# One inference layer on one core: the output projection's first operands loaded by the attention stage's SyncE, ahead of its last stores

## The chip, the cores and the metric

The kernel runs on one core of a Trainium2 chip. The metric is the device time in microseconds (us) of one execution; the median of three runs stands for the kernel. The engines are TensorE (PE, its weight loads PEld), VectorE (DVE), ScalarE (ACT), GpSimd (POOL) and SyncE (SP), which only issues transfers (DMAs).

## The reference

One layer of a streaming encoder, for 2048 prompt frames and 64 new frames of a second stream, D = 1024 features, fp32:

```python
h = rms_norm(x, norm_attn)
qa, ka, va, qb, kb, vb = split(h @ w_in)             # QK norm; rotary for mixer B
A = softmax(qa ka^T * s + rel_bias) va               # 8 heads, own 64-chunk and 8 before
B = sink_softmax(qb kb^T * s, sinks) vb              # 8 heads, own 64-chunk and 2 before
x = x + concat(A, B) @ w_out                         # the "combining" stage
gate, up = split(rms_norm(x, norm_ffn) @ w_gate_up)
x = x + (silu(causal_conv3(gate)) * up) @ w_down     # d_ff = 2816
```

## The kernel before

The work runs in four stages, one after the other, and in each the five engines follow programs of their own that meet only in semaphores: `project` (the input projection, to about 465 us of the span), `attend` (the attention, to 903 us), `combine` (output projection, residual and norm, to 1111 us) and `ffn` (to the end). An fp32 operand goes through TensorE as a high and a low part in three products (hi·hi, hi·lo, lo·hi); ScalarE makes the high part, VectorE the low part by a subtraction.

**attend** walks through 17 token tiles n = 0 to 16 of 128 tokens (tile 16 holds the 64 new frames), each with 12 units and 4 groups of heads: groups 0 and 1 are mixer A, 2 and 3 mixer B. For a group PE does the product with the values (L994), spreads the reciprocals of the sums (L999) and so counts `pv_ok` up; DVE copies them (`copy_r`, L1141) and multiplies (`divide`, L1149) into the buffer `o_t[mixer]`, of which there is one for each mixer. Then SP stores that buffer to the DRAM tensor oT (`store(n, mixer)`, L849). `divide` of a mixer's first group of tile n must wait until the store of tile n-1 has landed, since it writes into the same buffer:

```python
if n and g % 2 == 0:
    dve.wait_ge(o_st[mixer], 16 * n)
```

The sums of tile n are finished while the scores of tile n+1 are already under way, so that DVE does the divide of group (16, 0) in step (16, 7), ahead of the maxima (L1117, L1119) of the units from (16, 8) on, which ACT's exponentials wait for. SP's program is a plain list: what stands in it behind a wait or a transfer is issued behind it. At its end stand the four stores (15, A), (15, B), (16, A), (16, B). The stage ends when the last store has landed and all engines have met in a barrier.

In `attend` the values `v` lie in SBUF as 16 tiles of 2560 B in each partition. Mixer A of tile 15 reads value tiles 11 to 15; tile 16 reads only 0 and 1 (the cache and the new frames).

**combine** walks through 3 blocks of 704 tokens (two halves j of 352 each) and 4 pairs i of output tiles. A pair is 96 matmuls of 128x352: 2 output tiles s, 2 halves, 8 slices k, 3 products. The first block's operands come by pieces: `load_half(q, j)` brings two slices of oT for half j (352 KB), `load_w(g)` the two weight tiles of pair g (2 x 512 KB), `load_x(0, q)` the residual (704 KB). ACT and DVE split them in this order: half piece k = 0, weight tile 0, pieces k = 1 to 7, weight tile 1, then the eight pieces of j = 1. The pieces of j = 1 take the place of those of j = 0's neighbours, so SP issues `load_half(q, 1)` as DVE gets through the low parts (`o_lo_ok`), each followed by `load_x(0, q)`, and then the weights of pair 1. In the meantime POOL prepares sums of the feed-forward's weights, with loads and stores of its own on its own queue.

The buffers that combine and ffn share are made by `Carry`: `work` (the oT pieces lie in its upper third), `w_raw`, `small` (gains and a matrix of ones), `x1`, `big`.

Of the kernel before, what the change touches and what calls it, by code (L numbers as in the profile page):

```python
# [20 lines left out]
F32 = mybir.dt.float32  # L21
# [5 lines left out]
P = 128  # L27
# [664 lines left out]
                prep.piece(n)  # L692


def attend(nc, passed, q_a, k_a, qk_b, v_all, ka_cache, kb_cache, va_cache, vb_cache, sinks, oT):

# [17 lines left out]
    with ExitStack() as ctx:  # L714
# [108 lines left out]
        @block.sync  # L823
        def _(sp):
            by_heads = "f (a p) n -> p (f a) n"

            def load(n):
                c, w = place(n)
                load_raw(sp, raw, q_a, k_a, qk_b, c, w, ld)
                sp.dma_start(v[0:w, own_tile(n), :], v_all[c:c + w, :]).then_inc(ld, 16)  # L830

            def load_cache():

                twice(sp, cache[:, 0:KV_A, :], ka_cache.rearrange(by_heads, p=HEAD), cache_ld)
                twice(sp, cache[:, KV_A:, :], kb_cache.rearrange("(a p) n -> p a n", p=HEAD), cache_ld)
                sp.wait_ge(pv_ok, GROUPS * (FULL + 1))
                sp.dma_start(v[:, CACHE, 0:PAIRS_A * P], va_cache).then_inc(cache_ld, 16)
                sp.dma_start(v[:, CACHE, PAIRS_A * P:], vb_cache).then_inc(cache_ld, 16)

            def load_b(n):  # L840
                c, w = place(n)
                twice(sp, raw_b[:, :, 0:w], qk_b[0:PAIRS_B, :, c:c + w].rearrange(by_heads, p=HEAD), ld_b)

            def store(n, mixer):

                c, w = place(n)
# [348 lines left out]

class Carry:

    def __init__(self, nc, ctx):
        m = Memory(nc, ctx, "carry")
        self.big = m.sbuf("big", [P, 2 * KD * BLOCK + 4 * KD * P], F32R)
        self.x1 = m.sbuf("x1", [P, KD, BLOCK])
        self.w_raw = m.sbuf("w_raw", [P, RAW_RING, P])
        self.work = m.sbuf("work", [P, 12 * BLOCK])
        self.small = m.sbuf("small", [P, SMALL[-1]])  # L1210
# [31 lines left out]
        return self.w[:, 8 * P * c:8 * P * (c + 1)].rearrange("p (a k n) -> p a k n", a=2, n=P)  # L1242


def combine(nc, kept, oT, xT, w_o, gains, all_ones, x1T, h2T, h_sums, w_gu,
            prep_range, w_quads, t_gu, t_dn):


# [7 lines left out]
    with ExitStack() as ctx:  # L1256
# [13 lines left out]
        z = [[m.psum(f"z{s}{i}", [P, 512]) for i in range(2)] for s in range(2)]  # L1270
        ms = kept.ms

        const_ld = m.sem("const_ld")
        o_ld, w_ld = ([m.sem(f"{n}{i}") for i in range(2)] for n in ("o_ld", "w_ld"))
        x_ld, half_ld = ([m.sem(f"{n}{c}") for c in range(PAIRS)] for n in ("x_ld", "half_ld"))
# [39 lines left out]
        def _(sp):  # L1315
# [2 lines left out]

            def load_w(g):
                for s in range(2):  # L1320
                    if g:
                        sp.wait_ge(w_lo_ok[s], g)
                    sp.dma_start(w_raw[s][:], w_o[g % PAIRS, s]).then_inc(w_ld[s], 16)

            def load_o(b, q):
# [5 lines left out]
            def load_half(q, j):  # L1331

                n = PAIRS * j + q
                if j:
                    sp.wait_ge(o_lo_ok, 2 * (n - PAIRS + 1))
                cols = slice(j * SUB, (j + 1) * SUB)
                sp.dma_start(half_raw(n), oT[2 * q:2 * q + 2, :, cols].rearrange("k p n -> p k n")).then_inc(half_ld[n % PAIRS], 16)

# [1205 lines left out]
def encoder_step(nc, a):  # L2544

    scratch = {name: nc.dram_tensor(f"{name}_scratch", shape, F32, kind="Internal").ap()
               for name, shape in (("q_a", (4, P, TOKENS)), ("rel_rows", (P, HEADS, 3 * P)), ("oT", (KD, P, TOKENS)),
                                   ("x1T", (KD, P, TOKENS)), ("h2T", (KD, P, TOKENS)))}
    t_gu = nc.dram_tensor("t_gu_scratch", (D_FF // P, 4, P, 2, KD // 2, P), F32, kind="Internal").ap()
    t_dn = [nc.dram_tensor(f"t_dn{p}_scratch", (KD // 2, P, 2, 1, 4, P) if size == 2 else (KD // 2, 4, P, 2, size // 2, P), F32, kind="Internal").ap()  # L2550
            for p, size in enumerate(PART_SIZES)]
    h_sums = nc.dram_tensor("h_sums_scratch", (N_BLOCKS, 4, P, KD // 2, SUB), F32, kind="Internal").ap()
    passing = ExitStack()
# [3 lines left out]
    attend(nc, passed, scratch["q_a"], a["k_a"], a["qk_b"], a["v_all"], a["ka_cache"], a["kb_cache"], a["va_cache"],  # L2557
           a["vb_cache"], a["sinks"], scratch["oT"])
    passing.close()
    with ExitStack() as ctx:  # L2560
        kept = Carry(nc, ctx)
        combine(nc, kept, scratch["oT"], a["xT"], a["w_o"], a["gains_ffn"], a["all_ones"], scratch["x1T"], scratch["h2T"],
                h_sums, a["w_gu"], PREPARED[2], a["w_quads"], t_gu, t_dn)
        ffn(nc, kept, scratch["h2T"], h_sums, scratch["x1T"], a["w_gu"], a["w_dn"], t_gu, t_dn, a["conv"], a["state"],
            a["yT"], a["gate_prompt"], a["gate_sample"])
# [96 lines left out]
```

## Time and profile before

| | |
|---|---|
| median of 3 runs | 2514.19 us (2508.5 to 2514.99) |
| profiled execution | 2510.97 us, its span 2509.1 us |
| busy: PE, DVE, ACT, POOL | 95%, 68%, 46%, 40% |
| mean granted TensorE clock | 0.983 of 2.4 GHz |
| DMA | 578.24 MB, mean 230 GB/s |

Times inside the profile are us from the span's start. "Busy" is the share of the span in which an engine had an instruction under way. A wait is put down to the engine or transfer that released it. The transfers' time to landing runs from the issue to the last completion.

### The profile page before, as it was taken

Reading aid. Unit: us, or ns where it says so; the run is one execution under the profiler, and the core shown is the slowest. Engines: PE = TensorE matmul, PEld = TensorE weight load, DVE = VectorE, ACT = ScalarE, POOL = GpSimd, SP = SyncE. Lnnn points to the kernel's source line nnn. Section 1 sums busy time; section 2 is a strip of 40 time slices with the busy share of each in tenths; the row PEclk is TensorE's granted clock in tenths of the full one; section 3 lists DMA queues with packets and bytes.
Section 4 is the critical chain, followed back from the end, with each engine's and each line's share of the span. In section 5 each row is a group of like instructions: output and inputs, shape, how many; then the busy total and the mean of one; then the engine's idle time right before and its main releaser. Section 6 shows DMA issues by size and latency. Waiting matters only on the chain. (4 is left out here: it accounts for less than half of the span.)

```text
span 2509.1 us, 44859 instructions
## 1 busy us (share of the span) xinstructions
PE 2385.6 (95%) x15773; PEld 2236.7 (89%) x15773; DVE 1706.2 (68%) x3540; ACT 1159.6 (46%) x2656; POOL 992.1 (40%) x1145
## 2 busy tenths in 40 slices
PE   7999999799898979989999999999999999999997
PEld 5888888678787869988999999989999998999997
DVE  7656666576665656777766667777666677676665
ACT  6232332487676743344434344543344454344343
POOL 3888888668988868811310000123000021000001
PEclk9999999899999989999999999999999999999999
DMA  7776776866776668987786666968666686666665
GB/s 258 233 232 204 215 225 188 218 162 176 205 195 177 171 239 307 320 324 275 261 271 221 210 217 227 330 222 294 214 218 213 216 295 234 220 216 211 219 212 176
DMA packets 320939, 578.24 MB, mean 230 GB/s; under 512 B 35474, under 2 KB 168962, under 8 KB 320594
## 3 DMA queue, kind: packets, MB, share of 16 engines
q1 hardware_dynamic: 280560, 425.89, 53.1%
q0 software_dynamic: 39728, 149.36, 18.6%
q8 instruction: 124, 2.03, 0.3%
q14 instruction: 93, 0.76, 0.1%
q10 hardware_dynamic: 434, 0.20, 0.0%
HBM read 444.81 MB, written 132.10 MB: 230 GB/s over the span
## 5 line engine op out<-in xcount | busy, mean ns | idle before, releaser
L2170 PE MATMUL ffn_x<-carry_big 128*128 128x352 f32 x2508 | 457.7, 324 | 12.2 <-PEq L62 5.5
L2170 PEld LDWEIGHTS ffn_x<-carry_big 128*128 128x128 f32 x2508 | 409.6, 189 | 18.6 <-issue 13.6
L2170 PE MATMUL ffn_z<-ffn_h_hi_S,carry_big 128*128 128x352 f32 x1056 | 278.0, 326 | 16.4 <-DVE carry_big L2315 10.0
L366 PE MATMUL project_z<-project_w_hi,project_h_hi 128*128 128x512 f32 (+3 forms) x680 | 256.3, 377 | 14.9 <-DVE project_w_lo L539 11.5
L2069 POOL TENSOR_TENSOR carry_x<-carry_x,carry_work 128x352 f32<-128x352 f32 x48 | 52.2, 1088 | 507.5 <-DVE carry_work L2433 449.1
L366 PE MATMUL project_z<-project_w_lo,project_h_hi 128*128 128x512 f32 (+3 forms) x680 | 252.8, 372 | 0.0
L366 PE MATMUL project_z<-project_w_hi,project_h_lo 128*128 128x512 f32 (+3 forms) x680 | 252.5, 371 | 0.0
L2315 DVE TENSOR_TENSOR carry_big<-carry_w_raw,carry_big 128x512 fp32r<-128x512 f32 (+2 forms) x413 | 227.7, 559 | 0.9 <-ACT carry_big L2251 0.7
L2063 POOL DMA_DIRECT2D carry_work<-h_sums_scratch x8 | 4.4, 554 | 565.5 <-DVE ffn_y_lo_S L2337 561.0
L2170 PEld LDWEIGHTS ffn_z<-ffn_h_hi_S,carry_big 128*128 128x128 f32 x1056 | 188.1, 189 | 22.7 <-DVE carry_big L2315 22.5
L2251 ACT ACTIVATE carry_big<-carry_w_raw 128x512 fp32r<-128x512 f32 (+2 forms) x413 | 196.1, 502 | 6.2 <-PEq L62 4.6
L2170 PE MATMUL ffn_z<-ffn_h_lo_S,carry_big 128*128 128x352 f32 x528 | 170.5, 323 | 0.0
L2208 ACT ACTIVATE carry_work<-ffn_x 128x352 f32<-128x352 f32 x138 | 64.1, 464 | 215.3 <-PE ffn_x L2170 215.1
L366 PEld LDWEIGHTS project_z<-project_w_hi,project_h_hi 128*128 128x128 f32 (+1 forms) x680 | 126.9, 187 | 40.0 <-DVE project_h_lo L532 9.5
L2170 PE MATMUL ffn_x<-ffn_y_hi_S,carry_big 128*128 128x352 f32 x528 | 152.7, 326 | 9.9 <-DVE carry_x L2408 6.2
L2213 ACT ACTIVATE carry_work<-ffn_x 128x352 f32<-128x352 f32 x138 | 64.2, 465 | 203.9 <-PE ffn_x L2170 203.9
L2170 PE MATMUL ffn_z<-ffn_y_hi_S,carry_big 128*128 128x352 f32 x528 | 150.6, 323 | 0.0
L366 PEld LDWEIGHTS project_z<-project_w_hi,project_h_lo 128*128 128x128 f32 (+1 forms) x680 | 126.8, 186 | 24.9 <-issue 0.8
L963 PE MATMUL attend_s<-attend_keys,attend_q_hi 128*128 128x320 f32 (+4 forms) x368 | 134.4, 369 | 14.7 <-DVE attend_q_lo L1157 7.9
L138 POOL TENSOR_TENSOR passed_quads<-passed_quads 128x512 fp32r<-128x512 f32 x110 | 144.7, 1316 | 8.8
L366 PEld LDWEIGHTS project_z<-project_w_lo,project_h_hi 128*128 128x128 f32 (+1 forms) x680 | 127.0, 187 | 22.0 <-issue 0.8
L82 PE MATMUL combine_z<-combine_o_hi,carry_big 128*128 128x352 f32 x512 | 129.5, 333 | 15.2 <-DVE carry_big L1542 12.2
(249 smaller groups left out, 6458.1 us busy)
## 6 DMA issues: line engine op xcount, KB each, us to landing
carry_big<-t_gu_scratch SPq DMA_DIRECT2D x264, 512.0 KB, 4.0
carry_big<-t_dn_scratch SPq DMA_DIRECT2D x240, 256.0 KB, 3.3
carry_w_raw<-w_gu SPq DMA_DIRECT2D x198, 256.0 KB, 4.1
t_gu_scratch<-passed_quads POOLq DMA_DIRECT2D x88, 512.0 KB, 4.8
passed_quads<-w_quads POOLq DMA_DIRECT2D x110, 256.0 KB, 4.4
carry_w_raw<-w_dn SPq DMA_DIRECT2D x180, 128.0 KB, 3.4
carry_w_raw<-w_o SPq DMA_DIRECT2D x24, 512.0 KB, 6.1
t_dn_scratch<-passed_quads POOLq DMA_DIRECT2D x22, 512.0 KB, 4.4
```

The source lines that it names most:

```text
L82: last = nc.tensor.matmul(out, w_parts[w](k), act_parts[a](k), start=(k == 0 and (w, a) == PASSES[0]), stop=(k == n_k - 1 and (w, a) == PA ...
L138: pool.tensor_tensor(lo, four, hi.bitcast(F32), ALU.subtract).then_inc(self.lo_ok, 1)
L366: last = nc.tensor.matmul(z[c][0:w, 0:width], h[:, k, 0:w], ww[:, k, first:first + width], start=(k == 0 and h is hi and ww is w_hi), stop ...
L963: last = nc.tensor.matmul(ps[:, bank, 0:width], q[:, query, :], keys[:, key, c + first:c + first + width], start=q is q_hi and not begun, ...
L2063: pool.dma_start(h_source(b, name), src).then_inc(h_ld[H_STAGE[name]], 16)
L2069: nc.gpsimd.tensor_tensor(total, total, part[:], ALU.add).then_inc(done, 1)
L2170: mm = nc.tensor.matmul(bank[:, 0:SUB], weights(c)[:, wp, k, :], (hi, lo)[a][name][:, 1 if short else k, :], start=first and k == 0 and (w ...
L2208: nc.scalar.activation(sum2[g % 2][:], x_ps[g % 2][:, 0:SUB], ACT.Copy).then_inc(sum2_ok, 1)
L2213: nc.scalar.activation(sum3[g % 2][:], x_ps[g % 2][:, 0:SUB], ACT.Copy).then_inc(sum3_ok, 1)
L2251: nc.scalar.activation(weights(c)[:, 0], raw(c), ACT.Copy)\
L2315: nc.vector.tensor_tensor(weights(c)[:, 1], raw(c), weights(c)[:, 0].bitcast(F32), ALU.subtract).then_inc(w_lo_ok, 1)
```

## The change

A class `Ahead` claims the SBUF places of `x1`, `work`, `w_raw` and `small` at the very start of memory and frees them again at once, so that the other stages may use them; `Carry` later puts a block `reserved` over the same bytes and uses Ahead's views. (`big` and combine's own buffers thus move to other addresses; nothing else of them changes.) By the sizes in the code the pieces of oT then lie over value tiles 5 to 10 of `attend`, the two weight tiles and the small tensors over value tiles 10 to 13.

The eight loads that stood at the head of combine's SP program (four pieces `load_half(q, 0)`, the two weight tiles of pair 0, gains, ones) now stand in attend's SP program between store (14, B) and store (15, A), behind a wait for `pv_ok` = 64 (the four groups of tile 15) and for the stores of tiles up to 14. Combine's semaphores for these loads are made before both stages and cleared after combine.

```diff
 # attend, SP
                 if n == CACHE_TILE - 1:
                     load_cache()
+            sp.wait_ge(pv_ok, GROUPS * TILES)
+            for mixer in range(2):
+                sp.wait_ge(o_st[mixer], 16 * (TILES - 1))
+            ahead.load(sp, oT, w_o, gains, all_ones)
             for n in (TILES - 1, TILES):
                 for mixer in range(2):
                     store(n, mixer)
...
+class Ahead:
+    def __init__(self, nc):
+        with ExitStack() as before:
+            self.x1, self.work, self.w_raw, self.small = (
+                before.enter_context(nc.sbuf_tensor(f"ahead_{name}", shape, F32)) for name, shape in (
+                    ("x1", [P, KD, BLOCK]), ("work", [P, 12 * BLOCK]), ("w_raw", [P, RAW_RING, P]), ("small", [P, SMALL[-1]])))
...
+    def load(self, sp, oT, w_o, gains, all_ones):
+        half = lambda q: self.work[:, (8 + q) * BLOCK:(9 + q) * BLOCK].rearrange("p (a n) -> p a n", a=2)
+        for q in range(KD // 2):
+            sp.dma_start(half(q), oT[2 * q:2 * q + 2, :, 0:SUB].rearrange("k p n -> p k n")).then_inc(self.half_ld[q], 16)
+            if q == 0:
+                for s in range(2):
+                    sp.dma_start(self.w_raw[:, s * KD:(s + 1) * KD, :], w_o[0, s]).then_inc(self.w_ld[s], 16)
+        sp.dma_start(self.small[:, SMALL[1]:SMALL[2]], gains).then_inc(self.const_ld, 16)
+        sp.dma_start(self.small[:, SMALL[0]:SMALL[1]], all_ones).then_inc(self.const_ld, 16)
...
 # combine, SP
-            load_half(0, 0)
-            load_w(0)
-            for q in range(1, PAIRS):
-                load_half(q, 0)
-            sp.dma_start(g_in[:], gains).then_inc(const_ld, 16)
-            sp.dma_start(ones_sb[:], all_ones).then_inc(const_ld, 16)
             for q in range(PAIRS):
                 load_half(q, 1)
                 load_x(0, q)
```

On SP, at the end of attend's program (`attend_o_t0` and `attend_o_t1` are the buffers of mixers A and B, `ahead_work` receives the pieces of oT, `ahead_w_raw` the weight tiles):

```order
 L175 DMA attend_raw_b<-qk_b 64x8x64 x2
 L849 DMA oT_scratch<-attend_o_t1 128x4x128
+L1219 DMA ahead_work<-oT_scratch 128x2x352
+L1222 DMA ahead_w_raw<-w_o 128x1024 x2
+L1219 DMA ahead_work<-oT_scratch 128x2x352 x3
+L1223 DMA ahead_small<-gains_ffn 128x8
+L1224 DMA ahead_small<-all_ones 128x128
 L849 DMA oT_scratch<-attend_o_t0 128x4x128
 L849 DMA oT_scratch<-attend_o_t1 128x4x128
```

The eight loads went in ahead of the two stores of tile 15; the stores of tile 16 follow those.

On SP, at the head of combine's program before the change (`carry_work` are the pieces of oT, `carry_x` the residual):

```order
L1337 DMA carry_work<-oT_scratch 128x2x352
L1323 DMA carry_w_raw<-w_o 128x1024 x2
L1337 DMA carry_work<-oT_scratch 128x2x352 x3
L1371 DMA carry_small<-gains_ffn 128x8
L1372 DMA carry_small<-all_ones 128x128
L1337 DMA carry_work<-oT_scratch 128x2x352
L1341 DMA carry_x<-xT 128x2x704
```

and with the change:

```order
L1362 DMA ahead_work<-oT_scratch 128x2x352
L1366 DMA ahead_x<-xT 128x2x704
L1362 DMA ahead_work<-oT_scratch 128x2x352
L1366 DMA ahead_x<-xT 128x2x704
L1362 DMA ahead_work<-oT_scratch 128x2x352
```

The stage now begins with the pieces of j = 1 and the residual. The other engines' programs keep their order.

## Rows read from the trace of the kernel before

**Rows 1.** The page, busy time of each engine.

```profile
PE 2385.6 (95%) x15773; PEld 2236.7 (89%) x15773; DVE 1706.2 (68%) x3540; ACT 1159.6 (46%) x2656; POOL 992.1 (40%) x1145
```

**Rows 2.** Stretches of combine: length; busy PE, PEld, DVE, ACT, POOL; clock; DMA share; GB/s.

```profile
903.25:905.00 1.75, 0.00 (x0) 0.00 (x0) 0.06 (x1) 1.28 (x1) 1.10 (x2) 0.50 0.28 62
905.00:911.00 6.00, 0.19 (x1) 0.19 (x2) 2.00 (x3) 1.94 (x3) 0.55 (x1) 0.50 1.01 383
911.00:919.00 8.00, 7.03 (x22) 5.95 (x23) 6.58 (x8) 4.62 (x10) 7.22 (x10) 0.50 0.96 306
919.00:927.00 8.00, 7.79 (x46) 7.12 (x44) 5.14 (x7) 1.68 (x5) 7.25 (x9) 0.99 1.02 390
927.00:934.25 7.25, 5.50 (x24) 5.50 (x25) 4.44 (x6) 1.87 (x3) 5.25 (x6) 0.76 1.03 405
...
943.00:1050.00 107.00, 107.00 (x667) 106.57 (x666) 73.07 (x75) 36.55 (x44) 91.94 (x101) 1.00 0.90 312
```

**Rows 3.** Waits of PE, 910 to 1111: total us, times, longest.

```profile
PE combine_z L82 <- DVE carry_big L1542: 12.2, 2, 11.8
```

**Rows 4.** Timeline of SP's issues: start, length, line, transfer, count.

```profile
876.05 0.37 SPq L849 DMA_DIRECT2D oT_scratch<-attend_o_t  x1
...
894.26 0.36 SPq L849 DMA_DIRECT2D oT_scratch<-attend_o_t  x1
...
899.99 0.36 SPq L849 DMA_DIRECT2D oT_scratch<-attend_o_t  x1
903.25 0.36 SPq L1337 DMA_DIRECT2D carry_work<-oT_scratch  x1
903.66 0.94 SPq L1323 DMA_DIRECT2D carry_w_raw<-w_o  x2
...
907.28 0.65 SPq L1372 DMA_DIRECT2D carry_small<-all_ones  x1
911.75 0.38 SPq L1337 DMA_DIRECT2D carry_work<-oT_scratch  x1
...
919.06 1.36 SPq L1323 DMA_DIRECT2D carry_w_raw<-w_o  x2
```

**Rows 5.** Timeline of the first splits and the first matmul of combine.

```profile
903.25 1.28 ACT L1454 ACT_TABLE_LOAD   x1 [5.80 <-PEq L62]
...
906.48 0.50 ACT L1465 ACTIVATE combine_o_hi<-carry_work 128x352 fp32r<-128x352 f32 x1 [1.95 <-DMA carry_work<-oT_scratch]
...
908.44 1.06 ACT L1460 ACTIVATE carry_big<-carry_w_raw 128x1024 fp32r<-128x1024 f32 x1 [1.46 <-DMA carry_w_raw<-w_o]
...
910.81 0.66 PE L82 MATMUL combine_z<-combine_o_hi,carry_big 128*128 128x352 f32 x1 [11.78 <-DVE carry_big L1542]
...
913.14 4.86 DVE L1548 TENSOR_TENSOR combine_o_lo<-carry_work,combine_o_hi 128x352 fp32r<-128x352 f32 x6 [1.42 <-ACT combine_o_hi L1465]
```

**Rows 6.** DMA issues of short windows: KB each, median us to landing.

```profile
oT_scratch<-attend_o_t SPq DMA_DIRECT2D x1, 256.0 KB, 2.9
...
carry_small<-all_ones SPq DMA_DIRECT2D x1, 64.0 KB, 7.5
...
carry_w_raw<-w_o SPq DMA_DIRECT2D x2, 512.0 KB, 13.1
```

**Rows 7.** Timeline of DVE near the attention's end.

```profile
881.59 0.42 DVE L1141 COPY attend_r_sb<-attend_o 128x256 f32<-128x256 f32 x1 [0.31 <-PE attend_o L999]
...
887.35 0.42 DVE L1149 TENSOR_TENSOR attend_o_t<-attend_o,attend_r_sb 128x256 f32<-128x256 f32 x1
...
887.88 0.69 DVE L1119 TENSOR_REDUCE attend_nmax<-attend_s 128x2 f32<-128x514 f32 x1
```

**Rows 8.** A wait of PE in the attention, and the stretches after it.

```profile
PE attend_s L959 <- POOL attend_q_lo L908: 7.0, 1, 7.0
...
769.00:772.00 3.00, 0.02 (x1) 0.03 (x2) 0.00 (x0) 0.00 (x0) 2.99 (x4) 0.50 0.78 195
772.00:775.50 3.50, 3.50 (x15) 3.06 (x15) 1.26 (x2) 0.62 (x1) 3.20 (x5) 0.50 0.75 202
```

More of the change, by code:

```diff
@@ L692, in _, with attend @@
                 prep.piece(n)
-def attend(nc, passed, q_a, k_a, qk_b, v_all, ka_cache, kb_cache, va_cache, vb_cache, sinks, oT):
+def attend(nc, passed, ahead, q_a, k_a, qk_b, v_all, ka_cache, kb_cache, va_cache, vb_cache, sinks, oT, w_o, gains, all_ones):
     TILES = SEQ // P
@@ L1194, in _, with __init__ @@
                 divide(TILES, g)
+class Ahead:
[4 more added lines that the diff above has]
+                    ("x1", [P, KD, BLOCK]), ("work", [P, 12 * BLOCK]), ("w_raw", [P, RAW_RING, P]), ("small", [P, SMALL[-1]])))
+        m = Memory(nc, ExitStack(), "ahead")
+        self.half_ld, self.w_ld = [m.sem(f"half_ld{q}") for q in range(KD // 2)], [m.sem(f"w_ld{s}") for s in range(2)]
+        self.const_ld = m.sem("const_ld")
+        self.sems = m.sems
+    def load(self, sp, oT, w_o, gains, all_ones):
[7 more added lines that the diff above has]
+        sp.dma_start(self.small[:, SMALL[0]:SMALL[1]], all_ones).then_inc(self.const_ld, 16)
 class Carry:
-    def __init__(self, nc, ctx):
+    def __init__(self, nc, ctx, ahead):
         m = Memory(nc, ctx, "carry")
+        m.sbuf("reserved", [P, KD * BLOCK + 12 * BLOCK + RAW_RING * P + SMALL[-1]])
+        self.x1, self.work, self.w_raw, self.small = ahead.x1, ahead.work, ahead.w_raw, ahead.small
         self.big = m.sbuf("big", [P, 2 * KD * BLOCK + 4 * KD * P], F32R)
[L1207 to L1210, printed above, removed]
         self.ms = m.psum("ms", [P, SUBS, 512])
@@ L1242, in weights, with combine @@
         return self.w[:, 8 * P * c:8 * P * (c + 1)].rearrange("p (a k n) -> p a k n", a=2, n=P)
-def combine(nc, kept, oT, xT, w_o, gains, all_ones, x1T, h2T, h_sums, w_gu,
+def combine(nc, kept, ahead, oT, xT, w_o, x1T, h2T, h_sums, w_gu,
             prep_range, w_quads, t_gu, t_dn):
@@ L1271, in combine @@
         ms = kept.ms
-        const_ld = m.sem("const_ld")
-        o_ld, w_ld = ([m.sem(f"{n}{i}") for i in range(2)] for n in ("o_ld", "w_ld"))
-        x_ld, half_ld = ([m.sem(f"{n}{c}") for c in range(PAIRS)] for n in ("x_ld", "half_ld"))
+        const_ld, w_ld, half_ld = ahead.const_ld, ahead.w_ld, ahead.half_ld
+        m.sems += ahead.sems
+        o_ld, x_ld = [m.sem(f"o_ld{i}") for i in range(2)], [m.sem(f"x_ld{c}") for c in range(PAIRS)]
         w_hi_ok, w_lo_ok = ([m.sem(f"{n}{s}") for s in range(2)] for n in ("w_hi_ok", "w_lo_ok"))
@@ L1320, in load_w @@
                 for s in range(2):
-                    if g:
-                        sp.wait_ge(w_lo_ok[s], g)
+                    sp.wait_ge(w_lo_ok[s], g)
                     sp.dma_start(w_raw[s][:], w_o[g % PAIRS, s]).then_inc(w_ld[s], 16)
@@ L1333, in load_half @@
                 n = PAIRS * j + q
-                if j:
-                    sp.wait_ge(o_lo_ok, 2 * (n - PAIRS + 1))
+                sp.wait_ge(o_lo_ok, 2 * (n - PAIRS + 1))
                 cols = slice(j * SUB, (j + 1) * SUB)
@@ L2552, in encoder_step @@
     h_sums = nc.dram_tensor("h_sums_scratch", (N_BLOCKS, 4, P, KD // 2, SUB), F32, kind="Internal").ap()
+    ahead = Ahead(nc)
     passing = ExitStack()
@@ L2556, in encoder_step @@
             scratch["q_a"], a["k_a"], a["qk_b"], a["v_all"], scratch["rel_rows"])
-    attend(nc, passed, scratch["q_a"], a["k_a"], a["qk_b"], a["v_all"], a["ka_cache"], a["kb_cache"], a["va_cache"],
-           a["vb_cache"], a["sinks"], scratch["oT"])
+    attend(nc, passed, ahead, scratch["q_a"], a["k_a"], a["qk_b"], a["v_all"], a["ka_cache"], a["kb_cache"], a["va_cache"],
+           a["vb_cache"], a["sinks"], scratch["oT"], a["w_o"], a["gains_ffn"], a["all_ones"])
     passing.close()
     with ExitStack() as ctx:
-        kept = Carry(nc, ctx)
-        combine(nc, kept, scratch["oT"], a["xT"], a["w_o"], a["gains_ffn"], a["all_ones"], scratch["x1T"], scratch["h2T"],
+        kept = Carry(nc, ctx, ahead)
+        combine(nc, kept, ahead, scratch["oT"], a["xT"], a["w_o"], scratch["x1T"], scratch["h2T"],
                 h_sums, a["w_gu"], PREPARED[2], a["w_quads"], t_gu, t_dn)
```

## The prediction

> **What bounds the kernel now.** The page comes first: PE is busy 95% of the span [rows 1], so time is won or lost only where PE stands still or runs at a lower clock. I then looked at PE's busy time by stretches around the edit, the border between the attention and the combining stage. The stage begins at 903.25 (call it S), when SP issues its first load and ACT its table load [rows 4, 5]. From 943 to 1050 PE is busy 107.00 of 107.00 us at clock 1.00 [rows 2]. So whatever PE has gained or lost by about 934 stays to the end, and what happens behind that point need not be followed. Before it PE is held up: nothing up to 910.81, then 22 matmuls in 8 us at clock 0.50, then 46 in 8 us, then 24 in 7.25 us with the clock at 0.76 on average [rows 2]. A pair has 96 matmuls; at the later pace (667 in 107 us, 0.16 us each) it would take 15.4 us, and it took from 910.81 to about 934, 23. The view of PE's waits names two on the low part of a weight tile: 12.2 us in all, 11.8 for the first [rows 3], so only 0.4 us for the weights of pair 1, at 934.25.
>
> The edit touches two places: the loads that PE waits for at the stage's start, and SP's list at the attention's end, where the stores of tile 15 are now behind them.
>
> **What the change gives.** It removes eight issues and 4 x 352 + 2 x 512 + 4 + 64 = 2500 KB (2.56 MB) from the stage's start. Before, the first piece arrives 3.2 us behind S (ACT starts on it at 906.48, having waited for the DMA), the weight tile at 908.44 [rows 5]. With the data there, ACT's order decides: table load 1.28, the piece 0.50, so the weight's high part begins at S + 1.78; from there to the first matmul it took 910.81 - 908.44 = 2.37 us [rows 5], all ACT and DVE work that stays. First matmul at S + 4.15 instead of S + 7.56: 3.4 us earlier.
>
> The second part of the gain is in the train of transfers behind it. The stretches from 905 to 934 have the DMA engines at 0.96 to 1.03 of their time [rows 2]. The first piece of j = 1 is issued at 911.75, S + 8.5; the weights of pair 1, the last of the train that PE needs, are issued at 919.06 and land 13.1 us later, at 932.2 [rows 4, 6], 20.4 us behind the first issue of the train. That first issue waits for DVE's low parts of two half-slices. After the change these are done one split behind the first matmul: S + 4.15 plus some 1.0 (six of them take 4.86 us [rows 5], 0.81 each, and the first ran next to the weight's) is S + 5.2, 3.3 us earlier. Moreover, the train no longer queues behind the rest of the first loads, the last of which (the ones, issued 907.28, landing after 7.5) landed at 914.8 [rows 4, 6], 3.0 us behind 911.75. I take 2.0 of these 3.0, since the end of them is small packets. The weights of pair 1 then come 3.3 + 2.0 = 5.3 us earlier against S; DVE's pace is no obstacle (six half-slices in 4.86 us, from S + 5.2 on, instead of S + 9.9). PE must also have got through pair 0 by then. It begins 3.4 earlier and waits less for the late pieces of j = 1, so it may keep its clock at 1.00 there, where before it fell to 0.76 on average [rows 2]. I take 5.0 us; the lower bound is the 3.4 of the first matmul, the upper 3.3 + 3.0 = 6.3.
>
> **What it costs.** Eight issues go to a place where SP waits otherwise. They can begin when `pv_ok` reaches 64, that is when PE has done the last group of tile 15: DVE starts its copy of it at 881.59 [rows 7]. The same eight took 903.25 to 907.93 to issue [rows 4], 4.7 us. So store (15, A), issued at 876.05 before, is issued at 886.3, and store (15, B) right behind. Who waits for store (15, A)? DVE's divide of group (16, 0), at 887.35 [rows 7], and behind it on DVE all the maxima of the last four units (the next starts at 887.88), then ACT's exponentials, then PE's transposes and value products; this is the attention's tail, with nothing behind it to hide in.
>
> When does that store land? It stands in SP's queue behind 2.56 MB. The nearest rows for one transfer behind others on this queue: the weights of pair 1 land 13.1 us after the issue with some MB ahead of them, where a store of 256 KB on a free queue takes 2.9 [rows 6]. So the queue is worked off in its order. From the rate: data flow some 1.7 us after the first issue (62 GB/s up to 905, then 383 [rows 2]), 2.56 MB at 383 GB/s are 6.7 us, so 881.6 + 1.7 + 6.7 = 890.0, and the store itself 2.9 - 1.7 = 1.2 more: 891.2. From the landing: the ones landed 914.8 - 903.25 = 11.5 us behind the first issue, with two loads of 256 KB of POOL (0.5 MB, 1.4 us) among them, which are not there at 881: 10.1, then 1.2 for the store, 892.9. The stall is 3.9 by the first and 5.5 by the second, 7.0 if nothing is taken off for POOL. I take 4.8. It is 0 only if a store could overtake.
>
> The Trainium skill's page "DMA: Bandwidth & Descriptors", section "Anatomy of one DMA — SWDGE (gpsimd) path", has a fit of 2.0 us plus bytes over 436 GB/s. For the 2.56 MB and the store's 0.26 MB that would be, as an estimate from that page, 8.5 us, a landing at 890.1 and a stall of 2.7 us; the sum below would be -0.7 instead of +1.4. The stretch from 905 to 911 shows 383 GB/s at full DMA share, so here the trace's rate decides.
>
> During such a stall PE runs dry a unit or two later. What that does to its clock the attention shows elsewhere: after a wait of 7.0 us the clock stood at 0.50, and the next 3.50 us of full PE work ran at it (1.2 GHz) before it was back at 1.00 [rows 8]. Half of 3.5 is 1.75 us of lost work. The tail is a chain that goes through PE only in part, so less is on the path, but a chain with gaps may keep the clock down longer. I take 1.6; bounds 0 (the clock holds, or PE is not on the path) and 3.5 (all of the time at 0.50 is lost).
>
> Store (15, B) lands about 1 us behind (15, A) and is wanted by the divide of (16, 2), over 6 us later, so it costs nothing; without that cover it would cost its own 1 us. The last stores (894.26 and 899.99 before [rows 4]) find an empty queue. The wait for the stores of tile 14 is past by then. Nothing new is computed, and no buffer in combine or ffn gets smaller.
>
> **Sum.** +4.8 + 1.6 - 5.0 = +1.4 us. Against the profiled execution, 2510.97 us (span 2509.1), this is 2512.4; that execution lies 3.2 below the median of the runs shown, 2514.19, against which it is 2515.6. I name 2515. With all bounds the one way it is 3.9 + 0 - 6.3 = -2.4, the other way 7.0 + 3.5 - 3.4 = +7.1.
>
> **Rivals.**
>
> *The store is not held up: faster by 4 to 6 us* (2508 to 2510). If the transfers of the store flowed beside the loads, or the loads were through by 887, the stall would be under 1 us and the gain of 5.0 to 6.3 would stand alone. From a stall below 5.0 us without clock loss on the net time is negative. Against it: 13.1 us for the weights behind others. For it: no row shows a store behind loads of this size, and DMA is nearly idle there otherwise. 0.25. On this the same page's section "Queues, rings and completion order" says that descriptors are consumed in ring order and that the completion comes only after every earlier write of that DMA engine; by that rule this rival falls away but for a faster drain.
>
> *The tail stays at the lower clock: slower by 4 to 8 us* (2518 to 2522). The wait is as long as in the 7.0 us case, and the tail, short pieces of PE between waits for ACT and DVE, does not bring the clock back until the stage's end. Up to 3.5 us for that, a stall of 5.5 to 7.0, a gain of 5: +4 to +5.5, with the gain at its lower bound +8. It decides from a loss of 12.5 us on to bring "slower by over 0.3%". 0.17.
>
> *The gain is eaten by the transfers: slower by 3 to 5* (2517 to 2519). The stage's start stays limited by the train, of which only the first issue moves (3.3), and PE, early but starved of pieces of j = 1, waits longer there. 6.4 - 3.4 or less = +3 to +5. 0.13.
>
> *The forecast*, stall and gain nearly equal, -2.4 to +3: 0.45.
>
> **Numbers.** A change of this kernel can be told from none at about 0.3%, 7.5 us. None of the cases reaches -7.5 unless the stall is nil, the gain at its bound and the runs' scatter (6.5 us between the three shown) adds to it; +7.5 wants the second rival at its end, or scatter. Faster 0.05, within 0.86, slower 0.09. The range takes in the cases of both signs and a part of the scatter: 2507 to 2522; the likeliest case's own is 2511 to 2518.
>
> **What would show it.** In the changed profile: the eight loads issued from about 881.6 to 886.3; store (15, A) at 886 with a landing of 5 to 7 us instead of 2.9; DVE idle before the divide at 887 for 4 to 6 us, released by the DMA of oT; clock 0.50 for some us in the tail; the stage's start at about 909.6; the first matmul 4.1 to 4.3 us behind it; PE without idle time from 25 to 27 us behind it (31 before). The prediction is wrong if DVE doesn't wait there, if the tail between that divide and the stage's start (15.9 us before) grows by more than 3.5, or if PE's unbroken work starts less than 3 us earlier against S.

## The result, and the profile after

| | before | changed |
|---|---|---|
| median of 20 runs, timed together | 2515.51 us | 2522.2 us |
| ratio, 95% interval | | 1.0032, 1.0022 to 1.0042 |
| profiled execution, its span | 2510.97 us, 2509.1 | 2532.61 us, 2530.8 |

By that ratio the changed kernel is slower by 8.0 us (5.5 to 10.6); the medians are 6.7 apart, the means 7.4. One disturbed run of 4723 us is left out of the ratio. The profiled execution of the changed kernel is the slowest of the others. Its total, 21.7 us above the one of before, is no measure of the change. It shows where things wait; sizes are taken below from 18 profiled executions.

The page of the changed kernel, busy time of each engine, against [rows 1]:

```profile
PE 2396.2 (95%) x15773; PEld 2246.6 (89%) x15773; DVE 1696.8 (67%) x3540; ACT 1156.9 (46%) x2656; POOL 989.9 (39%) x1145
```

The same matmuls take 10.6 us more of PE's time. The count is the same, so this is not more work; the mean granted clock of this execution is 0.980 against 0.983 before.

Timeline of SP's issues in the changed kernel (start, length, line, transfer, count), against [rows 4]:

```profile
888.99 0.36 SPq L1219 DMA_DIRECT2D ahead_work<-oT_scratch  x1
889.40 0.94 SPq L1222 DMA_DIRECT2D ahead_w_raw<-w_o  x2
890.38 1.75 SPq L1219 DMA_DIRECT2D ahead_work<-oT_scratch  x3
892.17 0.60 SPq L1223 DMA_DIRECT2D ahead_small<-gains_ffn  x1
892.82 0.74 SPq L1224 DMA_DIRECT2D ahead_small<-all_ones  x1
893.60 20.84 SPq L849 DMA_DIRECT2D oT_scratch<-attend_o_t  x4
922.33 0.36 SPq L1362 DMA_DIRECT2D ahead_work<-oT_scratch  x1
```

The loads leave at once with DVE's copy of tile 15's last group (889.00 below, 881.59 before [rows 7]), and store (15, A) follows 4.6 us later. The row of four stores covers 20.84 us, since those of tile 16 wait for their data.

DMA issues from 893.5 to 893.8, the window of that store (KB each, median us to landing), against [rows 6]:

```profile
oT_scratch<-attend_o_t SPq DMA_DIRECT2D x1, 256.0 KB, 6.1
```

It lands at 893.6 + 6.1 = 899.7, 10.7 us after the first load's issue. On a free queue it took 2.9 [rows 6]. Who waits for it, in the timeline of the changed kernel:

```profile
889.00 0.42 DVE L1145 COPY attend_r_sb<-attend_o 128x256 f32<-128x256 f32 x1 [0.31 <-PE attend_o L1003]
...
894.22 0.42 DVE L1145 COPY attend_r_sb<-attend_o 128x256 f32<-128x256 f32 x1 [0.58 <-PE attend_o L1003]
...
899.72 0.42 DVE L1153 TENSOR_TENSOR attend_o_t<-attend_o,attend_r_sb 128x256 f32<-128x256 f32 x1 [5.08 <-DMA oT_scratch<-attend_o_t]
...
900.86 0.48 ACT L1063 ACTIVATE attend_prob<-attend_s,attend_nmax 128x257 f32<-128x257 f32 x1 [5.84 <-DVE attend_rden L1130]
...
901.94 0.40 PE L958 MATMUL attend_s<-attend_mask_k,attend_mask_q 128*128 128x257 bf16 x1 [5.53 <-ACT attend_prob L1063]
```

Read it downwards: DVE stands 5.08 us in front of the divide of group (16, 0), with the transfer as releaser; ACT 5.84 behind DVE; PE 5.53 behind ACT. It is one stall seen three times, not three.

Before the change DVE's copy for this group began at 886.82 and the divide 0.53 us behind it, at 887.35 [rows 7], with no wait; here they are 5.50 apart.

Stretches of the changed kernel (length; busy PE, PEld, DVE, ACT, POOL; clock; DMA share; GB/s), against [rows 2]:

```profile
892.50:899.00 6.50, 3.91 (x44) 3.25 (x43) 1.54 (x4) 1.75 (x6) 5.89 (x8) 1.00 1.00 327
899.00:905.00 6.00, 3.06 (x15) 2.81 (x16) 2.38 (x5) 3.20 (x13) 3.92 (x6) 0.54 0.48 162
905.00:911.00 6.00, 5.53 (x63) 4.49 (x62) 2.28 (x7) 2.95 (x10) 0.00 (x0) 0.90 0.25 69
911.00:919.00 8.00, 1.53 (x24) 1.29 (x24) 1.17 (x4) 2.19 (x3) 1.10 (x2) 0.84 0.06 16
919.00:927.00 8.00, 5.62 (x19) 5.11 (x20) 7.43 (x10) 4.87 (x11) 5.63 (x6) 0.52 0.64 206
927.00:935.00 8.00, 7.12 (x43) 6.54 (x42) 5.20 (x6) 2.51 (x6) 6.74 (x9) 1.00 1.02 368
935.00:943.00 8.00, 6.30 (x35) 5.78 (x36) 3.70 (x8) 1.94 (x3) 6.63 (x9) 1.00 1.03 407
943.00:1050.00 107.00, 105.97 (x662) 105.25 (x661) 74.16 (x76) 37.28 (x45) 92.65 (x106) 1.00 0.90 309
```

After the stall the clock is 0.54 for about 6 us. The DMA engines are full up to 899 at 327 GB/s, while from 911 to 919, up to the stage's start, they are nearly idle. From 927 to 943 they are full again, with the train of j = 1's pieces, residual and pair 1's weights.

Start of the combining stage in the changed kernel, and PE's starts behind a wait, against [rows 5]:

```profile
917.33 1.28 ACT L1473 ACT_TABLE_LOAD   x1 [5.80 <-PEq L62]
...
921.38 0.66 PE L82 MATMUL combine_z<-combine_o_hi,carry_big 128*128 128x352 f32 x1 [8.26 <-DVE carry_big L1561]
...
935.22 0.43 PE L82 MATMUL combine_z<-combine_o_hi,carry_big 128*128 128x352 f32 x1 [0.53 <-DVE combine_o_lo L1567]
937.93 0.43 PE L82 MATMUL combine_z<-combine_o_hi,carry_big 128*128 128x352 f32 x1 [1.48 <-DVE combine_o_lo L1567]
944.40 0.43 PE L82 MATMUL combine_z<-combine_o_hi,carry_big 128*128 128x352 f32 x1 [1.02 <-DVE carry_big L1561]
```

S is 917.33 here. The first matmul is at S + 4.05 (7.56 before). PE's last wait is at S + 27.1, for the low part of a weight tile of pair 1; the stretch from 943 on has it busy 105.97 of 107.00 us, all but that wait. The waits of 0.53 and 1.48 are for low parts of the pieces of j = 1. The kernel before has such waits too. They stand in the same view as [rows 3], in the line below the one shown there, and the last of them in the timeline of before:

```profile
PE combine_z L82 <- DVE combine_o_lo L1548: 2.9, 3, 2.0
...
928.75 0.43 PE L82 MATMUL combine_z<-combine_o_hi,carry_big 128*128 128x352 f32 x1 [1.97 <-DVE combine_o_lo L1548]
...
1052.33 0.43 PE L82 MATMUL combine_z<-combine_o_hi,carry_big 128*128 128x352 f32 x1 [0.45 <-DVE carry_big L1542]
```

So before the change PE's last wait near the stage's start ended at 928.75, S + 25.5. The second wait for a weight tile in [rows 3] is not at 934.25 but at 1052.33. From 928.75 on PE had no wait but a lower clock: 0.76 on average from 927 to 934.25 [rows 2], where the changed kernel has 1.00 from 927 to 943. The last wait is therefore no measure of the gain. How far PE has come is one: DVE's 13th addition of the residual in the first block (of 16), which waits for PE's sums, before and in the changed kernel:

```profile
970.31 0.52 DVE L1563 TENSOR_TENSOR carry_x<-carry_x,combine_z 128x352 f32<-128x352 f32 x1 [1.58 <-PE combine_z L82]
...
979.18 0.52 DVE L1582 TENSOR_TENSOR ahead_x<-ahead_x,combine_z 128x352 f32<-128x352 f32 x1 [1.53 <-PE combine_z L82]
```

That is S + 67.1 and S + 61.8: 5.2 us earlier in this pair of executions. Over all 18 executions it is at S + 62.6 on average in the 8 with moved loads and at S + 66.7 in the other 10, 4.1 earlier.

### The profile page after: what moved, and what is told of

Its sections match the earlier page's. It is cut to its first block and busy times, and to the rows that moved or that the text cites. A ratio compares the mean times of both kernels' runs of the same rounds, so it can differ in the third digit from the quotient of the medians.

```text
span 2530.8 us, 44864 instructions
## 1 busy us (share of the span) xinstructions
PE 2396.2 (95%) x15773; PEld 2246.6 (89%) x15773; DVE 1696.8 (67%) x3540; ACT 1156.9 (46%) x2656; POOL 989.9 (39%) x1145
## 5 line engine op out<-in xcount | busy, mean ns | idle before, releaser
L2189 PE MATMUL ffn_x<-carry_big 128*128 128x352 f32 x2508 | 465.4, 327 | 11.5 <-PEq L62 5.9
L2189 PEld LDWEIGHTS ffn_x<-carry_big 128*128 128x128 f32 x2508 | 416.5, 191 | 18.3 <-issue 14.1
L2189 PE MATMUL ffn_z<-ffn_h_hi_S,carry_big 128*128 128x352 f32 x1056 | 281.7, 329 | 15.9 <-DVE carry_big L2334 9.3
L2088 POOL TENSOR_TENSOR ahead_x<-ahead_x,ahead_work 128x352 f32<-128x352 f32 x48 | 52.2, 1088 | 509.7 <-DVE ahead_work L2452 451.3
L2334 DVE TENSOR_TENSOR carry_big<-ahead_w_raw,carry_big 128x512 fp32r<-128x512 f32 (+2 forms) x413 | 227.6, 559 | 0.6 <-ACT carry_big L2270 0.4
L2270 ACT ACTIVATE carry_big<-ahead_w_raw 128x512 fp32r<-128x512 f32 (+2 forms) x413 | 195.8, 501 | 5.8 <-PEq L62 4.7
L2227 ACT ACTIVATE ahead_work<-ffn_x 128x352 f32<-128x352 f32 x138 | 63.9, 463 | 216.5 <-PE ffn_x L2189 216.5
L2232 ACT ACTIVATE ahead_work<-ffn_x 128x352 f32<-128x352 f32 x138 | 64.0, 464 | 215.6 <-PE ffn_x L2189 215.6
L366 PEld LDWEIGHTS project_z<-project_w_lo,project_h_hi 128*128 128x128 f32 (+1 forms) x680 | 127.2, 187 | 21.7 <-issue 0.8
L2189 PE MATMUL ffn_x<-ffn_y_hi_A,carry_big 128*128 128x352 f32 x528 | 143.0, 324 | 0.0
```

The costliest lines, as they stand in the source:

```text
L366: last = nc.tensor.matmul(z[c][0:w, 0:width], h[:, k, 0:w], ww[:, k, first:first + width], start=(k == 0 and h is hi and ww is w_hi), stop ...
L2088: nc.gpsimd.tensor_tensor(total, total, part[:], ALU.add).then_inc(done, 1)
L2189: mm = nc.tensor.matmul(bank[:, 0:SUB], weights(c)[:, wp, k, :], (hi, lo)[a][name][:, 1 if short else k, :], start=first and k == 0 and (w ...
L2227: nc.scalar.activation(sum2[g % 2][:], x_ps[g % 2][:, 0:SUB], ACT.Copy).then_inc(sum2_ok, 1)
L2232: nc.scalar.activation(sum3[g % 2][:], x_ps[g % 2][:, 0:SUB], ACT.Copy).then_inc(sum3_ok, 1)
L2270: nc.scalar.activation(weights(c)[:, 0], raw(c), ACT.Copy)\
```

## The experiments

Every kernel was timed in five rounds (11 or 12 runs) against the kernel before on the same chip; "mean" is the difference of the means with its standard error. The first four ran together, and so on by fours. Stages are read from one profiled execution of each: the attention from its first score matmul to S, combining from S to the first matmul of the feed-forward. A table of all is behind the last experiment.

**The change again, for its comparison with the next three** (nothing edited):

> The changed kernel once more, on the chip of the next three, for its stretches. Theory A (the tail costs more than the head gives back): from the divide of group (16,0) to the first load of combine some 17.6 us plus a wait of 5 us before that divide, against 15.9 and 0 before; first matmul 4.1 us behind the stage's start; combine shorter by 2 us only; ratio 1.001 to 1.003. Theory B (the new addresses of the shared buffers slow other stages too): besides this, the feed-forward stage is longer than before by 3 us or more; ratio 1.003 or more.

1.0033 (1.0018 to 1.0048), mean +7.8 ± 1.5 us. The result repeats in a new comparison, and the stall in its profiled execution of 2522.2 us span. The lines of DVE in it:

```profile
894.38 0.42 DVE L1145 COPY attend_r_sb<-attend_o 128x256 f32<-128x256 f32 x1 [0.58 <-PE attend_o L1003]
900.02 0.43 DVE L1153 TENSOR_TENSOR attend_o_t<-attend_o,attend_r_sb 128x256 f32<-128x256 f32 x1 [5.22 <-DMA oT_scratch<-attend_o_t]
```

**The new places alone.** The eight loads stand at the head of combine's program again, in Ahead's places:

```diff
 # attend, SP
-            sp.wait_ge(pv_ok, GROUPS * TILES)
-            for mixer in range(2):
-                sp.wait_ge(o_st[mixer], 16 * (TILES - 1))
-            ahead.load(sp, oT, w_o, gains, all_ones)
 # combine, SP
+            ahead.load(sp, oT, w_o, gains, all_ones)
             for q in range(PAIRS):
                 load_half(q, 1)
                 load_x(0, q)
```

> The new places of the buffers alone: Ahead, the reserved block and the semaphores as in the change, but the eight loads stay at the head of combine, as before. Theory A: same time as before, ratio 0.999 to 1.001. Theory B (addresses): 1.001 to 1.003, with the added time in the feed-forward stage.

1.0026 (1.0013 to 1.0039), mean +6.5 ± 1.2. This was not foreseen: with no load moved, nearly the whole loss seemed to be there, while attention (431.0) and combining (209.4) were as before (428.8, 210.2). It set off the runs on numbers, addresses and repeats below.

**The loads behind the stores of tile 15.**

```diff
 # attend, SP
+            for mixer in range(2):
+                store(TILES - 1, mixer)
             sp.wait_ge(pv_ok, GROUPS * TILES)
             for mixer in range(2):
                 sp.wait_ge(o_st[mixer], 16 * (TILES - 1))
             ahead.load(sp, oT, w_o, gains, all_ones)
-            for n in (TILES - 1, TILES):
-                for mixer in range(2):
-                    store(n, mixer)
+            for mixer in range(2):
+                store(TILES, mixer)
```

> The change with the eight loads behind both stores of tile 15 and ahead of those of tile 16. Theory A: the wait of 5 us and the clock's fall in the tail are gone and the gain at combine's head stays: 2 to 5 us faster than before, ratio 0.998 to 0.999, 7 to 8 us below the change. Theory B: above 1.000, as far as the addresses cost.

1.0005 (0.9992 to 1.0019), mean +1.1 ± 1.1, that is 6.7 below the change beside it. Attention 428.1, combining 205.6. DVE's timeline of this kernel has no wait for a transfer at the same divide:

```profile
890.01 0.42 DVE L1146 COPY attend_r_sb<-attend_o 128x256 f32<-128x256 f32 x1 [0.58 <-PE attend_o L1004]
890.54 0.43 DVE L1154 TENSOR_TENSOR attend_o_t<-attend_o,attend_r_sb 128x256 f32<-128x256 f32 x1
```

**SP's wait alone**, in the kernel before:

```diff
+            sp.wait_ge(pv_ok, GROUPS * TILES)
+            for mixer in range(2):
+                sp.wait_ge(o_st[mixer], 16 * (TILES - 1))
             for n in (TILES - 1, TILES):
```

> The kernel before with only the wait for pv_ok = 64 (and the stores of tile 14) ahead of store (15, A), no load moved. If the loads ahead of the store make the stall: the store is issued at about 881.6 instead of 876.05, lands by 884.5, before the divide at 887.4, no wait, ratio 0.999 to 1.001. Rival, that the wait itself delays the store too long: DVE waits at the divide, 1.001 or more.

1.0013 (0.9998 to 1.0027), mean +2.3 ± 1.4; attention 430.5, combining 210.1. SP issues the stores of tile 15 as soon as `pv_ok` allows:

```profile
884.79 1.27 SPq L849 DMA_DIRECT2D oT_scratch<-attend_o_t  x2
```

Store (15, A) lands after 2.3 us, at 887.1, and the divide at 890.54 does not wait. So the wait on `pv_ok` alone makes no stall. The loads then act in two ways, which this run takes away together: SP needs 4.6 us to issue them, and 2.56 MB stand in front of the store. An estimate from the rows of the changed kernel: issued at 893.60 on a free queue, the store would land 2.9 us later, at 896.5, and DVE is ready for the divide at 894.64. So 1.9 us of the stall would be there by the late issue alone, and 3.2 come from the bytes in front.

**Semaphore numbers alone.** The change makes seven semaphores early, by which all later ones get other numbers. In the kernel before:

```diff
+    for i in range(7):
+        nc.alloc_semaphore(f"spare{i}")
     passing = ExitStack()
```

> The kernel before with nothing but seven unused semaphores allocated first, so that all others have numbers higher by seven, as in the change. Theory C (the project stage's end depends on the shifted numbers, since that is all that the change alters there): POOL issues its last store of that stage at about 467 instead of 462 to 464, attention starts at about 480 instead of 474 to 476, ratio 1.001 to 1.003. Rival D (those 4 us are the scatter of single executions): 0.999 to 1.001, POOL's last store at 462 to 464 as often as at 467.

1.0002 (0.9989 to 1.0015), mean 0.0 ± 1.3. No cost of the numbers shows.

**Addresses alone.** In the kernel before, Carry's buffers in the order that the change gives them, by the sizes in the code at the same addresses:

```diff
-        self.big = m.sbuf("big", [P, 2 * KD * BLOCK + 4 * KD * P], F32R)
         self.x1 = m.sbuf("x1", [P, KD, BLOCK])
+        self.work = m.sbuf("work", [P, 12 * BLOCK])
         self.w_raw = m.sbuf("w_raw", [P, RAW_RING, P])
-        self.work = m.sbuf("work", [P, 12 * BLOCK])
         self.small = m.sbuf("small", [P, SMALL[-1]])
+        self.big = m.sbuf("big", [P, 2 * KD * BLOCK + 4 * KD * P], F32R)
```

> The kernel before with nothing but the order of Carry's buffers changed to that of the change (x1, work, w_raw and small below big), numbers of semaphores as before. Theory B (addresses cost): 1.001 to 1.003, the time in combine or the feed-forward stage. Theories C and D: 0.999 to 1.001.

1.001 (0.9995 to 1.0026), mean +2.7 ± 1.7: between the theories, not decided.

**Loads behind the stores, and the change, both with Ahead's semaphores made last** (so that attend's keep their numbers):

```diff
         o_st = [m.sem(f"o_st_{x}") for x in "ab"]
+        ahead.make_sems(nc)
```

> The loads behind the stores of tile 15 as in e2_behind_stores, and Ahead's semaphores made as the last ones of attend, so that project's and attend's own keep their numbers. Theory C: 0.997 to 0.999, 4 to 6 us below before. Rival D: same as e2_behind_stores, 0.998 to 1.001.

1.0001 (0.9988 to 1.0015), mean +0.2 ± 1.3; attention 429.0, combining 207.3.

> The change as it is, with Ahead's semaphores made as the last ones of attend. Theory C: the wait for store (15, A) stays and the early part of the surplus goes, ratio 1.000 to 1.002. Rival D or theory B: as the change, 1.002 to 1.004.

1.0027 (1.0014 to 1.004), mean +6.3 ± 1.3; attention 434.9, combining 205.5. Both agree with their twins in the first set, so numbers are out, and the 6.1 us between these two repeat the 6.7 there: the order of loads and stores is worth six to seven us.

**A place of its own** for mixer A's output of tile 16. The loads stay ahead of the stores, but the divide has nothing to wait for:

```diff
+        def o_of(n, mixer):
+            return v[:, 14, 0:KD // 2 * P].rearrange("p (a n) -> p a n", n=P) if (n, mixer) == (TILES, 0) else o_t[mixer][:]
 # store and divide use o_of(n, mixer) for o_t[mixer][:]
-                if n and g % 2 == 0:
+                if n and g % 2 == 0 and (n, mixer) != (TILES, 0):
                     dve.wait_ge(o_st[mixer], 16 * n)
```

> The change, with the loads ahead of the stores of tile 15 as they are; only the output of mixer A of tile 16 goes to a place of its own (value tile 14, dead by then), so that its divide needn't wait for store (15, A). Theory A (that wait makes the stall): DVE goes on without the 5 us of waiting, the clock in the tail stays at 1.00, attention from its first matmul to its end some 429 instead of 436 us, 6 to 7 us below the change: ratio 0.999 to 1.001. Rival (the traffic of the loads slows the tail in another way): ratio 1.002 or more.

1.001 (0.9997 to 1.0023), mean +2.3 ± 1.3; attention 431.9, combining 207.9. In its timeline the store is as late as in the change (two stores issued from 894.34), and the divide does not wait:

```profile
894.45 0.42 DVE L1148 COPY attend_r_sb<-attend_o 128x256 f32<-128x256 f32 x1 [0.58 <-PE attend_o L1006]
894.91 0.42 DVE L1156 TENSOR_TENSOR attend_v<-attend_o,attend_r_sb 128x256 f32<-128x256 f32 x1
```

**The kernel before against itself, the places again, the addresses again** (no new edits):

> The kernel before as a kernel of its own, nothing changed: what the comparison gives for no change. 0.9985 to 1.0015; its profile shows how the end of the project stage scatters (attention's first matmul at 474 to 478 by the scatter theory, at 474 to 476 by the others).

1.0009 (0.9999 to 1.0019), mean +1.8 ± 1.1. A comparison of one and the same program can come out 0.09% from 1.

> e1_places_alone once more, on another chip. If the claim of places costs some 4 to 6 us by itself: 1.0015 or more again. If e1's ratio was scatter: 0.999 to 1.001.

1.0016 (1.0004 to 1.0028), mean +3.5 ± 1.5: about half of the first comparison, and 1.7 above the unchanged program beside it.

> e5_addresses_alone once more. If the other addresses of the shared buffers are what costs in e1_places_alone: 1.001 to 1.003. If not: 0.999 to 1.001.

1.0015 (1.0004 to 1.0026), mean +4.2 ± 1.0, 2.4 above the unchanged program beside it.

**Four more side by side:** places, the kernel before, the change, and the place of its own, each a repeat.

> The new places of the first operands, with their loads left at the head of the combining stage (the third comparison of this program; the two before gave +6.5 and +3.5 us in the mean). Theory that the reserved places alone cost time: 2 us or more above the unchanged program that is timed beside it in this set. Rival, that the two comparisons only scattered: within 1.5 us of that unchanged program. In the profile, in both: attention about 429 us long and the combining stage about 210 us.

1.0012 (0.9998 to 1.0025), mean +2.9 ± 1.4, 5.0 above the unchanged program beside it.

> The kernel before, unchanged, compared with itself (the second such comparison; the first gave 1.0009). Both theories: a ratio of 1.000 within 0.001. What it differs from 1 by is what a comparison of this set gives for no change, and the three beside it are read against it.

0.9989 (0.9978 to 1.0), mean -2.1 ± 1.2: off by as much as the first control, to the other side.

> The change as it is, the third comparison. Theory that only the held-up store and the clock behind it cost time (about +7 us of attention against a gain of about 3 us in the combining stage): +4 us, and 4 to 5 us above the version with a place of its own beside it plus what that version gains. Theory that the places cost 2 to 4 us more: +6 to +8 us.

1.0019 (1.0006 to 1.0032), mean +5.1 ± 1.5. PE's wait for the exponentials at that place is 4.9 us; in the change's other executions it is 5.5, 5.7 and 6.0.

> The change, with the first mixer's output of tile 16 in a place of its own, so that its divide waits for no store. Theory of the stall alone: 3 us faster than before, since the gain in the combining stage is left with no stall against it. Theory that the places cost 2 to 4 us: no difference from before. Both: 5 to 7 us faster than the change beside it, and attention 430 us long in the profile.

0.999 (0.9972 to 1.0007), mean -1.8 ± 1.6, which is 7.0 below the change beside it and about that of the unchanged program. The gain in combining (205.7) is there, and yet it does not show. Stretches of this kernel at the attention's end, columns as above, show what the stall does to the clock, by its absence:

```profile
892.50:899.00 6.50, 5.73 (x59) 4.89 (x59) 4.14 (x9) 4.28 (x17) 5.89 (x8) 1.00 1.01 339
899.00:905.00 6.00, 4.94 (x65) 3.99 (x63) 2.54 (x7) 4.06 (x12) 4.02 (x6) 1.00 0.59 174
```

The same DMA load stands in the same stretch (339 and 174 GB/s against 327 and 162), and the clock stays at 1.00 where the changed kernel has 0.54. So it is the stall that costs the clock, not the transfers.

**All stages, us, of one profiled execution each**

| kernel | first score matmul at | attention | combining | from there to the end |
|---|---|---|---|---|
| before | 474.4 | 428.8 | 210.2 | 1395.7 |
| before, 2 repeats | 474.9, 479.4 | 429.4, 429.3 | 209.9, 211.3 | 1394.6, 1397.4 |
| numbers; wait alone | 477.7, 475.9 | 429.1, 430.5 | 210.2, 210.1 | 1392.8, 1399.3 |
| addresses, 2 | 475.5, 479.6 | 427.9, 432.0 | 209.8, 211.8 | 1398.7, 1396.9 |
| places, 3 | 479.9, 474.7, 477.3 | 431.0, 428.2, 430.7 | 209.4, 210.1, 212.7 | 1397.7, 1397.3, 1397.2 |
| behind stores, 2 | 478.4, 477.7 | 428.1, 429.0 | 205.6, 207.3 | 1395.9, 1394.8 |
| own place, 2 | 479.0, 479.6 | 431.9, 431.1 | 207.9, 205.7 | 1399.0, 1398.4 |
| the change, 4 | 480.9, 479.8, 480.6, 478.0 | 436.4, 437.9, 434.9, 439.1 | 208.2, 207.4, 205.5, 204.1 | 1405.3, 1397.1, 1397.3, 1396.0 |

Two columns split without overlap. Attention: 437.1 on average where the divide waits (4 executions, 434.9 to 439.1), 429.8 where it does not (14, 427.9 to 432.0), +7.3. Combining: 206.5 where its first loads were moved (8, up to 208.2), 210.5 where they were not (10, from 209.4), -4.1. The part of the attention that the edit touches is sharper than the whole: from DVE's copy for group (16, 0) to S it is 16.4 us in all 14 executions without the wait, and 22.9 to 23.7 in the 4 with it, +6.8 on average. The other 0.5 of the +7.3 arose earlier in the stage. The other two columns overlap: one and the same program (before, three executions) has its first score matmul from 474.4 to 479.4.

## Why the prediction was wrong, by its own steps

**The mechanism was right, and it is shown.** Loads in front, a store held up in SP's queue, DVE at the divide of (16, 0), PE behind it, a lower clock, an earlier first matmul: each stands in the trace. Two edits that each break one link (the loads behind the stores; an own place for what the divide writes) take the stall away, and on the same chip they came out 6.7, 6.1 and 7.0 us below the change. The wait alone brings no stall. The rival "the store is not held up" fell. The last load, issued at 892.82, landed 6.2 us later, at 899.0, and the store at 899.7, behind it. The Trainium skill's page "DMA: Bandwidth & Descriptors", section "Queues, rings and completion order", says that each DMA engine consumes descriptors in ring order and that the completion comes only after its earlier writes; the trace agrees. The fit in that page's section "Anatomy of one DMA — SWDGE (gpsimd) path", of the same Trainium skill, gives 8.5 us for loads and store, as an estimate; here the store landed 10.7 us behind the first load's issue.

**The stall, predicted 4.8:** 5.08, and 5.22, 5.50 and 4.49 in the three repeats. Right.

**The clock, predicted 1.6:** from the divide to the stage's start 917.33 - 899.72 = 17.6 us, 15.9 before: 1.7, and 1.8 to 2.1 in the repeats. Both terms together are the +6.8 from DVE's copy to S, predicted 6.4. Right.

**The gain, predicted 5.0: mis-sized, the smaller of the two steps that failed.** It is 4.1 on average, by the length of combining and by the 13th addition alike. The first matmul came 3.5 earlier against S, as worked out (3.4). The second part did not come in full. The pieces of j = 1 are issued at S + 5.0, as I said (5.2), 3.4 earlier than in the executions without moved loads (S + 8.4 on average). But the weights of pair 1, which I had 5.3 us earlier, reach ACT at S + 24.6 on average against S + 28.4, 3.8 earlier. The train behind its first issue became 0.4 us shorter and not 2.0; the DMA engines are full from 927 to 943. There was a misreading too: I put the last 0.4 us of [rows 3] at 934.25, as a wait for these weights. It is at 1052.33, so in the profiled execution before the change PE was held there by the pieces of j = 1 and by its clock, not by the weights. In the changed kernel it does wait for them (1.02 at 944.40; 1.1, 0.3 and nothing in the repeats). The gain lies between the rival "the gain is eaten by the transfers" (3.4) and the forecast (5.0). With measured sizes the two places give +6.8 - 4.1 = +2.7 us (predicted +1.4, the rival +3).

**What the prediction costed at nothing: the new places. This step carried the time out of the range.** All it says of them is "Nothing new is computed, and no buffer in combine or ffn gets smaller"; that `big` and combine's own buffers move to other addresses got no term, no rival and no reason for zero. In the comparisons, by means against the kernel before, the standard errors combined over the repeats:

| what | mean, us | places by the sum |
|---|---|---|
| same program, or other numbers (3 comparisons) | -0.1 ± 0.7 | |
| places alone (3) | +4.3 ± 0.8 | 4.3 |
| behind stores (2): places - 4.1 | +0.6 ± 0.8 | 4.7 |
| own place (2): places - 4.1 | +0.2 ± 1.1 | 4.3 |
| the change (3, without the 20 runs of the result): places + 2.7 | +6.4 ± 0.8 | 3.7 |
| addresses alone (2) | +3.4 ± 1.0 | |

Four kinds of kernel, each with the stages' differences taken off, leave about 4 us that go with the places. It would explain why the versions without the stall, which have the gain of 4 us in the trace, are no faster than before. It shows only in many runs together: the three comparisons of the places alone gave 6.5, 3.5 and 2.9, and the two pure controls lay 1.8 and -2.1 off. That is more than their standard errors (1.1 and 1.2), so the error of the 4.3 is rather 1.2 than 0.8, an estimate from the two controls. Addresses alone came out at much of it, which points to where buffers lie in SBUF; but that order was one try. How an address costs time stays open.

The granted clock moves with it: its mean over the runs of the places alone is 0.9818, 0.9827 and 0.9828, against 0.9831, 0.9835 and 0.9830 of the kernel before beside them, and among the runs of the kernel before 0.001 less clock goes with 1.6 us more. Whether the clock is a cause here or follows from waits elsewhere is not shown. No row shows a place where the time goes: in the profiled executions of before, repeats, numbers and wait alone, the first score matmul is at 476.5 on average, in the eleven with the new places at 478.7; from the feed-forward's first matmul to the end it is 1396.0 and 1397.8 (1397.1 without the slowest, 1405.3). Each of these differences of up to 2 us is about as large as one execution's scatter (2 to 3 us), and the input projection, where the first lies, uses none of the moved buffers. So the cause of this term stays open.

**The sum in hindsight:** 2515.5 (the median of before in the larger set, 1.3 above that of the three runs) + 2.7 + 4.3 = 2522.5; measured 2522.2. Of the 7.2 us between forecast and result, 1.9 are the base and rounding, 1.3 the mis-sized terms (0.9 the gain, 0.4 stall and clock), the other 4.0 the places. Without them the sum is 2518.2, well inside the range. The forecast's sign for the edit's own effect was right, and the chance of 0.09 for "slower" too small, since its cases held only mechanisms around the moved loads and no loss elsewhere.

**Tests named ahead:** issues of the loads with DVE's copy, taking 4.6 us: as said (4.7). Landing 6.1: in 5 to 7. DVE idle 5.08: in 4 to 6. Stage start: not comparable, since this execution was 7.4 us late already at 889.00. First matmul S + 4.05, said 4.1 to 4.3. PE unbroken at S + 27.1, said 25 to 27; its mark before, 31, was the misreading (25.5 by the trace). Of the three signs of being wrong, DVE did wait, and the tail grew by 1.7, less than 3.5. The third, by PE's unbroken work, tests nothing, since its mark was wrong. None of the three looked at the places, where the prediction failed.

## What to carry to other kernels

Before a prefetch is put into an in-order queue, look at what stands behind it and who reuses the buffer of those stores: 2.56 MB ahead of a store of 256 KB made SP issue it 4.6 us later, turned its landing from 2.9 into 6.1 us and stopped three engines in turn; the same loads behind the store cost nothing there. A load that starts earlier is worth only what the train behind it lets through, so move the second transfer in thought too. And when a change also moves buffers, time the placement by itself, with the unchanged kernel as a control beside it: here it came out at about as much as the effect under study, and no version that moved the loads beat the kernel before.

## What was not expected of the hardware

- Between three executions of the unchanged program the end of the input projection differs by 5.0 us (474.4, 474.9, 479.4), and the latest of them also has the longest span (2517.4 against 2509.1 and 2508.8). A single pair of profiled executions can tell a wait, not a change of 0.3%.
- Five rounds of one program against itself gave 1.0009 and 0.9989.
- The order of buffers in SBUF alone measured 1.001 (0.9995 to 1.0026) and 1.0015 (1.0004 to 1.0026), and the new places 1.0012 to 1.0026, with no wait in the trace that explains it.
